# Attention of two transformer blocks on one core: scores, transposes and value products issued by pairs of heads

## The reference, cut to what matters

```python
scores = jnp.einsum('bdhnqe,bdhnke->bdhnqk', qb, kb) * (e ** -0.5)
scores = jnp.where(mask, scores, NEG_INF)
m = jnp.max(scores, axis=-1)
p = jnp.exp(scores - m[..., None])
den = jnp.sum(p, axis=-1)
o = jnp.einsum('bdhnqk,bdhnke->bdhnqe', p, vb) / den[..., None]
```

## Time and profile before

| | us |
|---|---|
| median of 3 runs | 2987.16 |
| lowest and highest run | 2985.3, 2987.48 |
| span of the profiled execution | 2985.3 |
| PE busy / weight loads / DVE / ACT / POOL | 2778.3 / 2214.1 / 1387.5 / 631.0 / 883.6 |
| four attention stages, first to last score | 217, 204, 188, 265 |

### The profile page before, as it was taken

One profiled execution on the slowest core, in us unless ns is written; L12 is line 12 of the kernel. 1 busy time (PEld: TensorE's weight loads), 2 busy tenths in 40 slices (PEclk: granted clock), 3 DMA queues, 4 the chain that ended last, 5 costly groups with the idle time before them and its releaser, 6 DMA issues.

```text
span 2985.3 us, 33951 instructions
## 1 busy us (share of the span) xinstructions
PE 2778.3 (93%) x12436; PEld 2214.1 (74%) x12436; DVE 1387.5 (46%) x2577; ACT 631.0 (21%) x1495; POOL 883.6 (30%) x862
## 2 busy tenths in 40 slices
PE   6799999999999998959898899998988999999995
PEld 2487778977799776738686777777767888888884
DVE  1411346977668675671543612224363334434435
ACT  3212222122311233440122022230141100110111
POOL 0541213323142322313343412214213433333330
PEclk8899999999999999979998999999989999999997
DMA  5410112112221222533332121214241111111112
GB/s 170 127 53 27 59 48 74 58 55 78 73 77 53 69 86 92 187 132 120 113 125 71 36 75 60 64 59 174 78 127 43 52 48 46 53 42 56 42 63 99
DMA packets 155597, 236.11 MB, mean 79 GB/s; under 512 B 24764, under 2 KB 69564, under 8 KB 155464
## 3 DMA queue, kind: packets, MB, share of 16 engines
q1 hardware_dynamic: 155464, 234.35, 24.3%
HBM read 181.65 MB, written 52.64 MB: 78 GB/s over the span
## 4 chain that ended last, share of the span: by engine, by line
PE 87%; DVE 7%; DMA 3%; issue 1%; POOL 1%; ACT 1%; SPq 0%; POOLq 0%; DVEq 0%; ACTq 0%
PE ps L1673 50%; PE ps L1829 12%; PE ps L1842 12%; PE ps L1731 5%; PE ps L1741 3%; PE ps L1755 3%; PE ps L1685 2%; PE ps L1702 2%; DVE act_lo L1196 1%; DVE scr L1283 1%; DMA small<-st_d 1%; DVE act_lo L1504 1%; DMA scr<-x_d 1%; POOL w_lo L860 1%; DMA scr<-in_x 0%
## 5 line engine op out<-in xcount | busy, mean ns | idle before, releaser
L858 POOL CAST w_hi<-raw 128x512 fp32r<-128x512 f32 x416 | 311.5, 749 | 2012.4 <-DMA raw<-in_w_in 932.1
L1673 PE MATMUL ps<-act_hi,w_hi 128*128 128x512 f32 x1344 | 558.2, 415 | 50.4 <-DVE act_lo L1196 46.5
L860 POOL TENSOR_TENSOR w_lo<-raw,w_hi 128x512 fp32r<-128x512 f32 x416 | 580.2, 1395 | 33.3
L1673 PE MATMUL ps<-act_lo,w_hi 128*128 128x512 f32 x1344 | 533.3, 397 | 0.0
L1673 PE MATMUL ps<-act_hi,w_lo 128*128 128x512 f32 x1344 | 531.2, 395 | 0.0
L1283 DVE SCALAR_TENSOR_TENSOR scr<-scr,small 128x512 f32<-128x512 f32 x480 | 420.6, 876 | 11.5
L1673 PE MATMUL ps<-w_hi,act_hi 128*128 128x512 f32 (+1 forms) x960 | 386.8, 403 | 6.7 <-DVE act_lo L1196 6.6
L1673 PE MATMUL ps<-w_lo,act_hi 128*128 128x512 f32 (+1 forms) x960 | 376.4, 392 | 0.0
L1673 PE MATMUL ps<-w_hi,act_lo 128*128 128x512 f32 (+1 forms) x960 | 376.3, 392 | 0.0
L1673 PEld LDWEIGHTS ps<-act_hi,w_hi 128*128 128x128 f32 x1344 | 257.2, 191 | 104.5 <-issue 56.5
L1673 PEld LDWEIGHTS ps<-act_lo,w_hi 128*128 128x128 f32 x1344 | 256.0, 190 | 57.6
(11 more groups left out here) (166 smaller groups left out, 3111.4 us busy)
## 6 DMA issues: line engine op xcount, KB each, us to landing
raw<-in_w_in SPq DMA_DIRECT2D x176, 256.0 KB, 3.1
raw<-in_w_up SPq DMA_DIRECT2D x64, 256.0 KB, 2.6
raw<-in_w_down SPq DMA_DIRECT2D x64, 256.0 KB, 2.6
vreg<-in_w_ada SPq DMA_DIRECT2D x48, 256.0 KB, 3.5
raw<-in_w_in SPq DMA_DIRECT2D x72, 128.0 KB, 2.2
x_d<-big SPq DMA_DIRECT2D x16, 512.0 KB, 3.0
scr<-x_d SPq DMA_DIRECT2D x16, 512.0 KB, 4.4
o_d<-scr SPq DMA_DIRECT2D x48, 128.0 KB, 2.0
```

Source lines behind the costliest of these rows:

```text
L858: pool.tensor_copy(dhi, src).then_inc(w_hi_done, 1)
L860: pool.tensor_tensor(dlo, src, dhi.bitcast(F32), ALU.subtract).then_inc(w_ready, 1)
L1673: ins = nc.tensor.matmul(out_, lhs, rhs, start=(m == 0), stop=(m == 3 * nk - 1))
```

## The change

Two heads now go through together. A pair p (32 of them in a stage) is heads 2i and 2i+1 in the first three groups, and i and i+4 in the second block, so that one lies in the lower and the other in the upper 64 partitions. A pair's two scores stand directly behind one another, into `ps_s[0]` and `ps_s[1]`. All its transposes (4 or 2) go to the one bank `ps_t`, and one ACT copy moves them to `probT`, which has become a single buffer of 512. All value products (8 or 4 instructions) go to the one bank `ps_o`, and one DVE copy of 128 columns moves them out. `ps_s`, `prob`, `ps_t`, `probT` and `ps_o` each hold one pair only: `score_max` of a pair waits for the transposes of the pair before. The pair's three PE parts are all in the same pair step, no longer a step or two apart, and the projections are cut around them by `pair_fill`: 2, 12 and 4 matmuls in groups 0 to 2, and 3, 15 and 6 in group 3, in this order: first part, scores, second part, transposes, third part, value products.

```diff
+def pair_fill(C, p):
+    per = att_share(C)
+    a, b = 2 * p * per, 2 * p * per + 2 * per
+    return a, a + 2 * per // 8, b - 2 * per // 4, b
...
-        probT = [scr[:, 512 + i * 256:512 + (i + 1) * 256] for i in range(2)]
+        probT = scr[:, 512:1024]
...
+        def pair_heads(g, p):
+            i = p % 4
+            return (2 * i, 2 * i + 1) if g < NG else (i, i + 4)
...
+            def probs_out(g, p):
+                n = att_cfg(g, p // 4)[1]
+                act.wait_ge(probs_t, 32 * g + p + 1)
+                if 32 * g + p >= 1:
+                    act.wait_ge(pv, 32 * g + p)
+                both = lambda t: t.rearrange("p (j k) -> p j k", j=2)[:, :, 0:n]
+                nc.scalar.activation(both(probT), both(ps_t), ACT.Copy).then_inc(pt_out, 1)
...
+            def att_pair(g, p):
+                us = att_units(g)
+                a, b, c, d = pair_fill(len(ATT_STAGES[g]), p)
+                for i in units_in(a, b):
+                    f_unit(us[i])
+                for j in range(2):
+                    exps(g, p, j)
+                for i in units_in(b, c):
+                    f_unit(us[i])
+                probs_out(g, p)
+                for i in units_in(c, d):
+                    f_unit(us[i])
...
-                for s in range(66):
-                    if s < 64:
-                        score_max(g, s)
-                    if s >= 2:
-                        out_head(g, s - 2)
-                    if s < 64:
-                        for i in units_done(C, s):
-                            f_unit(us[i])
-                        if g < NG:
-                            conv_taps(("step", g, s))
+                for p in range(32):
+                    a, b, c, d = pair_fill(C, p)
+                    for i in units_in(a, b):
+                        f_unit(us[i])
+                    if p >= 1:
+                        out_pair(g, p - 1)
+                    for j in range(2):
+                        score_max(g, p, j)
+                    for i in units_in(b, d):
+                        f_unit(us[i])
+                    conv_taps(("step", g, 2 * p))
+                    conv_taps(("step", g, 2 * p + 1))
+                out_pair(g, 31)
...
-                for s in range(66):
-                    if s < 64:
-                        for m in range(s * per, (s + 1) * per):
-                            proj(us[m // 24], m % 24)
-                        score(g, s)
-                    if 1 <= s < 65:
-                        prob_t(g, s - 1)
-                    if s >= 2:
-                        prob_v(g, s - 2)
+                for p in range(32):
+                    a, b, c, d = pair_fill(len(ATT_STAGES[g]), p)
+                    for m in range(a, b):
+                        proj(us[m // 24], m % 24)
+                    score_pair(g, p)
+                    for m in range(b, c):
+                        proj(us[m // 24], m % 24)
+                    turn_pair(g, p)
+                    for m in range(c, d):
+                        proj(us[m // 24], m % 24)
+                    value_pair(g, p)
```

More of the change, by code:

```diff
@@ L1117, in _ @@
                                      scale=c_ps[:, u[1]:u[1] + 1]).then_inc(free_of(u), 1)
[L1118 to L1128 removed]
+            for p in range(32):
+                att_pair(3, p)
+                if p % 4 == 1 and p > 1:
+                    act.wait_ge(y2_den, p // 4)
                     nc.scalar.activation(tiny[:, 8:16], tiny[:, 0:8], ACT.Exp).then_inc(y2_exp, 1)
+            act.wait_ge(y2_den, NB)
+            nc.scalar.activation(tiny[:, 8:16], tiny[:, 0:8], ACT.Exp).then_inc(y2_exp, 1)
             for B in range(NB):
@@ L1720, in qkv_unit, with score_pair @@
                     project(u)
-            def score(g, s):
-                a = 64 * g + s
-                B, h = s // 8, s % 8
+            def score_pair(g, p):
+                B = p // 4
                 k0, n, _ = att_cfg(g, B)
[L1726 to L1741, removed]
[L1742 to L1757 removed]
+                if 32 * g + p >= 1:
+                    pe.wait_ge(att_max, 64 * g + 2 * p)
@@ new lines, in score_pair, with turn_pair @@
+                for j in range(2):
+                    rows = slice(64 * j, 64 * j + 64)
+                    keys = kT[rows, p % 4, k0:k0 + n] if g < 3 else kT2[rows, k0:k0 + n]
+                    nc.tensor.matmul(ps_s[j][:, 0:n], qT[rows, p % 4, P * B:P * B + P], keys, start=True, stop=True
+                                     ).then_inc(scores, 1)
+            def turn_pair(g, p):
+                n = att_cfg(g, p // 4)[1]
+                pe.wait_ge(probs, 64 * g + 2 * p + 2)
+                if 32 * g + p >= 1:
+                    pe.wait_ge(pt_out, 32 * g + p)
+                for j in range(2):
+                    for i in range(n // P):
+                        ins = nc.tensor.transpose(ps_t[:, 256 * j + P * i:256 * j + P * i + P],
+                                                  prob[j][:, P * i:P * i + P], ident[:, :])
+                ins.then_inc(probs_t, 1)
@@ new lines, in value_pair @@
+            def value_pair(g, p):
+                k0, n, _ = att_cfg(g, p // 4)
+                pe.wait_ge(pt_out, 32 * g + p + 1)
+                if 32 * g + p >= 1:
+                    pe.wait_ge(o_out, 32 * g + p)
+                for j in range(2):
+                    h = pair_heads(g, p)[j]
+                    for i in range(n // P):
+                        v = (V[:, k0 // P + i, 64 * h:64 * h + 64] if g < 3
+                             else V2[:, k0 // P + i, 64 * (h // 4):64 * (h // 4) + 64])
+                        ins = nc.tensor.matmul(ps_o[:, HD * j:HD * j + HD],
+                                               probT[:, 256 * j + P * i:256 * j + P * i + P], v, start=(i == 0),
+                                               stop=(i == n // P - 1))
```

127 lines of the change are left out of this document (50 added, 77 removed).

## The result

| | before | after |
|---|---|---|
| median of 4 runs on one chip, us | 2987.32 | 2913.73 |
| lowest and highest run | 2985.3, 2988.4 | 2913.16, 2917.26 |
| span of the profiled execution | 2985.3 | 2911.7 |
| ratio, 95% interval | | 0.9756, 0.9743 to 0.977 |

The change takes 73.6 us off, where 28.5 were forecast. The direction is right, the size is not: 2913.7 lies under the range's lower end of 2943, and under the 2944 that rival (a) ended at.

A forecast was written before the change was run, and what follows sets the result against it. PE's instruction list was taken to bound the attention stages. Pairing saves 35 us and stage ends 4; group 3's start adds 2, late maxima 4.5, value products 4: 28.5 less, 2958.7 us on the median, range 2943 to 2977.

The forecast's parts named there:

- rival (a): Scores of a pair: the two heads' streams overlap by 0.11 to 0.21 with 256 keys; 2944 to 2951 us, chance 0.30.
- 0.40 once, and two streams, 0.85 or 0.43: Scores of a pair on PE: sides paid once plus both heads' streams, 1.25 us with 256 keys or 0.83 with 128.
- The bound of 0.21 less: Second head's score in a pair: at most 0.21 us below the sum, if the halves overlap; 0 was taken.
- (b): Between a pair's scores: the second head's weight load stands bare, 128 x 0.11 = 14 us back; 2973 us, chance 0.12.
- (c): Between a pair's scores: changing halves drains the array, 0.20 a pair, 26 us back; 2984 us, chance 0.11.
- (d): Between a pair's scores: changing halves costs 0.40, 51 us in all, so slower; 3010 us, chance 0.07.
- The sides: Around a pair's scores on PE: 0.40 us that is no streaming, paid once a pair.
- The stage ends: End of attention stages: PE's waits of 0.75 and 0.41 us for copies go; 4 us less in all.
- Late maxima: PE standing before transposes because DVE's units and taps delay the next maximum, groups 1 and 2; 4.5 us more (0 to 12).
- Group 3's start: PE waits before the first transposes behind DVE's DMA-held first maximum; 2 us more, some 5 us idle.
- Value products waiting for the 512-column copy: Value products some 0.1 us late in 44 pairs of groups 0 and 1 with 256 keys; 4 us more (0 to 9).
- The cover of the transposes: Transposes possible 2.5 us after a pair's first score row, PE there at 3.9: no wait, 1.4 us to spare.

The follow-up runs named there:

- same-half kernel: Changed kernel with heads paired so both lie in the same half of the partitions, all else kept; 2956.27 us, ratio 0.9896 to the kernel before.
- taps first: Changed kernel, DVE taking a unit that ends in the third part behind the pair's taps; 2905.71 us; with group 3's store wait also moved, 2899.29 us.
- scores only: Kernel before with one edit: scores of steps s and s+1 issued together at even s; 2916.49 us, ratio 0.9764.

## Why the prediction was wrong

**The failed step** is "0.40 once, and two streams, 0.85 or 0.43", with "I take 0, since the second pass within a head is the nearest row". That row is of one half of the rows, and for one half it holds: the same-half kernel has the second head's passes 0.216 apart. For two halves no row existed, and there the second head adds nothing: the pair's block costs 0.83 and not 1.25 with 256 keys, and 0.21 less than the sum has with 128. The bound of 0.21 less was too small as well for 256 keys, and with 128 the rival had "nothing, since there the loads fill the time".

**Rival (a)** had the mechanism and not the size. It let streams overlap but kept "loads of 0.11 one after another". The trace has the loads 7 ns apart. That gave 8 to 15 us for 43, and put the range's end 29 us too high. (That end, 2943, was called the lower middle of (a), but (a) went from 2944 to 2951, so it lay just under it.) Full overlap of streams and loads would have given 2958.7 - 43 = 2916. I weighed (a) against a row that could not show two halves at all, and gave it 0.30. The Trainium skill (TensorEngine Tiling, Tiling Modes, Key Properties) says that tiles can load and multiply in parallel; the trace now agrees with both halves of that, 7 ns for loads and 7 ns for passes.

**Rivals (b), (c), (d)**, which cost 14 to 51 us for going from one half to the other, fall with the same row: the change of halves costs 7 ns.

**The rest of the sum** stands in the main, and the same-half kernel checks it: 31 us against 28.5. That the two are so near is in part luck. Its four stages are 35.5 us shorter together, and 4.4 are lost outside them; and the 4 us taken for value products that wait did not come.
- The sides: 0.40 once per pair, 0.83 for the block less 0.43. Transposes: 440.73 - 439.83 - 0.46 = 0.44, taken at 0.46. Value products: 442.58 - 441.20 - 0.46 = 0.92, taken at 0.90. A third block costs nothing, as said. The period of a 256-key pair in group 0 is 442.90 - 436.55 = 6.35 where 6.75 less 0.43 is 6.32.
- The stage ends: in after, no wait before transposes or value products stands where the earlier trace rows have 0.75 and 0.41, but what group 2's stage leaves earlier is waited for again behind it, as said. In these two profiles the 3.2 us under "all else" are mostly there: between groups 2 and 3, PE's waits for the stored outputs and for DVE (in the view of waits 8.0 and 7.3 us, before 6.6 and 5.3) grew by 3.4. But this stretch changes from one execution to the next: it is 560.0 us long in after and 555.9 before, and 553.8 and 561.4 in the two kernels with taps first, whose programs differ only behind it. So it is not shown that the change costs anything there.
- Late maxima: 4.5 taken, 5.8 measured. Group 2's two pairs are 1.5 each, near the 1.7 worked out. Group 1 has three waits and not one: 1.1 behind a glu unit and four taps (0.5 said), 0.2, and 1.5 in the stage's first pair, which four taps had no part in; its DVE had waited for a store before a first tap (see taps first).
- Group 3's start: some 5 said, 5.1 measured.
- Value products waiting for the 512-column copy: 4 taken, nothing found. In the pair above they start 0.23 behind the last projection, as an undisturbed instruction does. The copy is through at 441.29, 1.23 behind the start of the transposes, about as said; then come weights and the first value product:

```profile
441.34 0.97 PEld L1777 LDWEIGHTS ps<-vreg,scr 128*128 128x128 f32 x8 [0.19 <-ACT scr L1027]
441.43 1.02 PE L1777 MATMUL ps<-vreg,scr 128*128 128x64 f32 x8
```

  The load does wait for the copy, 0.19, but starts 0.09 ahead of the value product, and that was enough. The copy comes just in time, not 0.1 late.
- The cover of the transposes: chain 2.5 said, 2.35 measured; PE there at 3.9 said, 440.06 - 436.55 = 3.51 measured, since the scores' row is shorter. The slack is 1.16 and not 1.4, and it holds.

By stages, with 0.70 and 0.49 a pair, 1.2 at the ends of groups 0, 1 and 3, and the waits as measured, the sum gives 22.8, 17.4, 12.7 and 20.7, in all 73.6; measured are 23.1, 18.3, 13.6 and 21.8, in all 76.8, and 3.2 are lost elsewhere. The 3 us between the two sums, at most 1.1 a stage, stay open.

**Who earned it.** With scores only, groups 0, 1 and 2 save 23.7, 21.3 and 16.7, against 23.1, 18.3 and 13.6. The differences of 3.0 and 3.1 in groups 1 and 2 are the late maxima of 2.8 and 3.0. So joining transposes, value products and copies, and going to single buffers, brought nothing on PE that the stages show, and cost the slack that late maxima then used up, behind four taps or behind a late store. The two parts, joined copies and single buffers, were not tried one by one.

## What to carry over

In this kernel, f32 matmuls with a contraction of 64 belong next to each other in the list in twos, one in each half of the rows and each with a bank of its own: the second is then free with 128 and with 256 columns, while the same half or one full-height matmul between them loses that. Where a step's price is bounded by two rows far apart, look at which resource the row shares (here: one half of the array) before taking the nearest row, and keep the full overlap as an end of the range. Try the smallest edit that holds the mechanism first: here a few lines gave what the whole change gave, and left the buffers that hid the vector engine's delays.

## What the runs showed of the hardware

- Two heads' f32 scores from different row halves into different banks: first passes 7 ns apart, second passes too, and loads too, although in the same-half kernel both passes of the first head come before those of the second. It costs 0.64 for two heads with 256 keys and 0.42 with 128, the same as one head.
- Same half: the second head's passes start 0.216 us apart at 256 columns, and the pair costs 1.06 and 0.64.
- One full-height matmul between them: the pair's cost goes from 0.83 to 1.65, and each lone score has its 0.40 of sides.
- After PE had stood for 3.34 us at group 3's start, the granted clock was 0.50 from about 1.2 us behind the wait, and seven projections took 0.43 each and no longer 0.23.
